# Cross-attention of eight samples to memory: column groups of four samples at a time, key tiles in another order

## The chip, the cores and the metric

The kernel runs on one core of a Trainium2 chip. Its TensorE (PE) multiplies, VectorE (DVE), ScalarE (ACT) and GpSimd (POOL) work on vectors, and DMA queues move data between the chip's main memory and the core's own. The metric is the device time of one execution in microseconds (us).

## What is computed

One inference step of a two-layer decoder, for a prompt of 512 tokens and for eight samples of four tokens each. Both share all weights. Every layer has a token mixer, a cross-attention with four heads into 256 memory rows, and a feed-forward block. The change lies in the cross-attention of the samples. Each sample has its own keys and values, given as inputs (`cache_mem_k`, `cache_mem_v`), and its tokens attend to all 256 of them:

```python
def gqa_attend(q, k, v, mask):
    b, tq, h, dh = q.shape
    g = k.shape[2]
    qg = q.reshape(b, tq, g, h // g, dh)
    s = jnp.einsum('btgod,bsgd->bgots', qg, k).astype(jnp.float32) * (dh ** -0.5)
    s = jnp.where(mask, s, NEG_INF)
    p = jnp.where(mask, jax.nn.softmax(s, axis=-1), 0.0)
    o = jnp.einsum('bgots,bsgd->btgod', p.astype(v.dtype), v)
    return o.reshape(b, tq, h, dh), p

def cross_attend(h, mk, mv, wq, wo):
    b, t, _ = h.shape
    q = (h @ wq).reshape(b, t, XATTN_HEADS, XATTN_HEAD_DIM)
    o, _ = gqa_attend(q, mk, mv, True)
    return o.reshape(b, t, D_MODEL) @ wo
...
        xs = xs + rmsnorm(cross_attend(rmsnorm(xs, gn[2]), cache_mem_k[li], cache_mem_v[li], w_xq[li], w_xo[li]), gn[3])
```

One sample has four heads of four tokens, 16 rows of queries. Its keys of one layer are 8 chunks of 128 by 256, its values 2 chunks of 128 by 1024: 1 MB each.

## The kernel before

The program is written by hand, one list of instructions for each engine, with semaphores between them. Each engine runs its list strictly in the written order.

**PE.** In a layer, `cross(l)` follows the query projection. It works on the prompt (`scores`, `turn`, `values`, in four blocks of 128 queries) and on the samples in turn. For the samples:

- Keys (L1938 to L1944). `xqd[:, b, c, :]` holds the queries of sample b, chunk c, in 32 columns: two samples share one 32-row strip of the result, each filling half of it and leaving zeros in the other. So the result of sample b goes to rows 32*(b//2) of `ps[.., 1, 0:256]`, and the strip sums 16 matmuls: 8 chunks of two samples. A strip of 32 result rows is a column group of PE's array, since the stationary operand has 32 columns. The order is sample by sample: 8 matmuls each, 64 in all, with a rise of `mk_used` after each sample.
- Softmax on DVE and ACT, transposes on PE, and ACT's copy to `xst` (L913).
- Values (`s_values(hb)`, L1915). For the four samples of a half, each in a strip of its own (rows 32*j), two matmuls for each half `f` of the 1024 columns, 512 wide. The order is sample by sample, 4 matmuls each, with a rise of `mv_used` after each. Between the two halves stand blocks 2 and 3 of the prompt's scores and some transposes.

**Tiles.** A key or value tile of a sample is loaded by POOL's DMA queue into one of six places (`NC` = 4 places in the ring `cring` and `XC` = 2 in free space). The list `TILES` (L166 to L173) gives the order of loading, and with it the place: the n-th tile of a layer's keys and values goes to place n mod 6. `tile(n)` waits until the tile before it in the place was used (`tile_used`, L524 to L535), then issues the DMA. POOL does this in the order of the list, between its sums for the norms: the first four tiles of a layer before the norm of the memory, the other twelve after the last projection of the memory's values. PE waits in `tile_in` for the tile's arrival (`cache_full`).

Weights come by another queue (SyncE) into a ring of four blocks. The blocks of the output projection that follows `cross` are requested up to its fourth before `cross` begins.

Of the kernel before, what the change touches and what calls it, by code (L numbers as in the profile page):

```python
# [34 lines left out]
P = 128  # L35
# [3 lines left out]
NB, NT = 8, 4  # L39
# [125 lines left out]
TILES = [("cmp", b, kv, h) for b in range(NB) for kv in "kv" for h in range(2)]  # L165
for _hb in range(2):  # L166
# [2 lines left out]
    TILES += [("win", _hb, "v", 0)]  # L169
    TILES += [("slc", 4 * _hb + j, "k", h) for j in range(2, 4) for h in range(2)]  # L170
    TILES += [("slc", 4 * _hb + j, "v", h) for j in range(4) for h in range(2)]
TILES += [("mem0", b, kv, 0) for kv in "kv" for b in range(NB)]
TILES += [("mem1", b, kv, 0) for kv in "kv" for b in range(NB)]  # L173
TILE = {t: i for i, t in enumerate(TILES)}

XC = 2
# [80 lines left out]
def decoder_step(nc, a, w, o):  # L257

    with ExitStack() as ctx:
# [13 lines left out]
        def S(name):  # L273

            if name not in sems:
                sems[name] = ctx.enter_context(nc.semaphore(name))
            return sems[name]
# [25 lines left out]
        ps = ctx.enter_context(nc.psum_tensor("ps", [P, 8, 512], F32))  # L303
# [66 lines left out]
        xqd = flatx[:, 1280:3328].rearrange("p (b c n) -> p b c n", b=NB, c=8)  # L370
# [69 lines left out]
        def tile_in(e, *t):  # L440

            n = TILE[t]
            e.wait_ge(cfull[PLACE[n]], 16 * TURN[n])
            return place_of(n)
# [71 lines left out]
        def _(pool):  # L516
# [6 lines left out]
            def tile_used(n):  # L523

                kind, b, kv, hh = TILES[n]
                if kind == "cmp":
                    pool.wait_ge(S("sub_ready"), n + 1)
                elif kind == "win":
                    pool.wait_ge(S("sw_sc" if kv == "k" else "sw_pv"), b + 1)
                elif kind == "slc" and kv == "k":  # L530
                    pool.wait_ge(S("kt_tr"), 4 * (2 * b + hh + 1))
                elif kind == "slc":
                    pool.wait_ge(S("sv_used"), 2 * b + hh + 1)
                else:
                    pool.wait_ge(S("mk_used" if kv == "k" else "mv_used"), 8 * int(kind[3]) + b + 1)  # L535

            def tile(n):
                kind, b, kv, hh = TILES[n]
# [37 lines left out]
            k = 0  # L576
            at = NC
# [994 lines left out]
        def _(pe):  # L1572
            pe.wait_ge(S("const_loaded"), 32)

            def mm(out, lhsT, rhs, start, stop, **kw):
                return pe.matmul(out, lhsT, rhs, start=start, stop=stop, **kw)  # L1576
# [83 lines left out]
            for kind, k in FIRST:  # L1660
# [3 lines left out]
                if kind == "in":  # L1664
                    last = plain(g, WSEG["w_in"][0] + k, h, 8, 0, KC, None if k else "h_ready")
# [212 lines left out]
            def cross(l):  # L1878
# [35 lines left out]

                def s_values(hb):  # L1915

                    for j in range(4):
                        b = 4 * hb + j
                        mv = tile_in(pe, f"mem{l}", b, "v", 0)
                        for f in range(2):  # L1920
                            for kt in range(2):
                                at = kt * P + 32 * (b // 2)
                                last = mm(ps[32 * j:32 * j + 32, 6 * hb + f, :], xst[:, at:at + 32],
                                          mv[:, kt * 1024 + 512 * f:kt * 1024 + 512 * f + 512], kt == 0, kt == 1)
                        last.then_inc(S("mv_used"), 1)

                def s_turn(hb):
                    pe.wait_ge(S("xv_copied_a"), 2 * l + hb + 1)
# [6 lines left out]
                scores(0)  # L1935

                pe.wait_ge(S("xq_apart"), l + 1)
                for b in range(NB):  # L1938
                    mk = tile_in(pe, f"mem{l}", b, "k", 0)
                    rows = slice(32 * (b // 2), 32 * (b // 2) + 32)  # L1940
                    for c in range(8):
                        last = mm(ps[rows, 1, 0:256], xqd[:, b, c, :], mk[:, c * 256:c * 256 + 256],
                                  b % 2 == 0 and c == 0, b % 2 == 1 and c == 7)
                    last.then_inc(S("mk_used"), 1)  # L1944
                scores(1)
                turn(0)
                pe.wait_ge(S("xs_norm"), l + 1)
# [195 lines left out]
```

## Time and profile before

| | |
|---|---|
| median of 3 runs | 2154.64 us (2154.55 to 2156.26) |
| span of the profiled execution | 2150.9 us |
| PE busy (share of the span), instructions | 1977.7 us (92%), 13423 |
| PE weight loads | 1734.4 us (81%) |
| VectorE | 1021.7 us (48%) |
| ScalarE | 710.4 us (33%) |
| GpSimd | 255.9 us (12%) |
| DMA queue of GpSimd (q0) | 109.53 MB, 13.7% of 16 engines |

The span is the time from the first to the last instruction of the one execution that was profiled. Its rows below are read from that execution. In them, a form such as "128*32 128x256" is a stationary operand of 128 rows by 32 columns and a moving operand of 128 by 256. `mc` is the memory that holds the ring and more, and stands for the tiles in both keys and values; `big` holds the queries (`xqd`) and the probabilities (`xst`); `kstore` is the prompt's keys, `vstore` its values, `cst` the identity for transposes, `small` other queries of the samples.

### The profile page before, as it was taken

What the parts mean: (1) busy time and instruction counts of PE and PEld (TensorE: products, weight loads), DVE (VectorE), ACT (ScalarE), POOL (GpSimd) and SP (SyncE); (2) the same over time, 40 slices, a digit from 0 to 9 for tenths busy, and PEclk for the clock granted to TensorE, in tenths of its full rate; (3) what the DMA queues carried; (4) which work ended last, traced back from release to release, by engine and by line L of the source; (5) the groups of instructions that cost most, each with busy time, mean ns of one, the idle gap of its engine ahead of it and who ended that gap; (6) DMA issues with size and microseconds to landing.
All of it is one profiled execution on the core that took longest, in us unless ns stands there. A gap on an engine that the chain in (4) does not pass through costs nothing.

```text
span 2150.9 us, 31915 instructions
## 1 busy us (share of the span) xinstructions
PE 1977.7 (92%) x13423; PEld 1734.4 (81%) x13423; DVE 1021.7 (48%) x1429; ACT 710.4 (33%) x1179; POOL 255.9 (12%) x231
## 2 busy tenths in 40 slices
PE   5997999898989997999999979898999899999995
PEld 4785764647979567999999979887965799999995
DVE  5994774242374225544432176755522364444213
ACT  2113553233452144322222232754313332222221
POOL 2340001110230003000000121021200210000011
PEclk8996999999999998999999989999999999999998
DMA  6893005554254511222222222243551222222221
GB/s 227 335 374 139 1 1 196 192 175 162 79 166 147 196 40 49 89 88 87 86 85 87 87 63 82 89 153 128 181 186 41 77 69 88 88 88 85 87 86 59
DMA packets 59656, 254.75 MB, mean 118 GB/s; under 512 B 10224, under 2 KB 10624, under 8 KB 45904
## 3 DMA queue, kind: packets, MB, share of 16 engines
q1 hardware_dynamic: 40320, 135.39, 19.6%
q0 software_dynamic: 14656, 109.53, 13.7%
q10 hardware_dynamic: 4576, 8.34, 1.1%
q8 instruction: 78, 1.28, 0.2%
q14 instruction: 26, 0.21, 0.0%
HBM read 244.89 MB, written 12.68 MB: 120 GB/s over the span
## 4 chain that ended last, share of the span: by engine, by line
PE 81%; DVE 12%; ACT 4%; DMA 1%; issue 1%; POOL 0%; SPq 0%; ACTq 0%; DVEq 0%; POOLq 0%
PE ps L1576 77%; DVE work L1102 3%; PE ps L1838 2%; DVE big L1163 1%; PE ps L1744 1%; DVE work_r L1124 1%; DVE rinv L1086 1%; DVE wring_r L1116 1%; ACT whi L677 1%; DVE x L1105 1%; ACT work L848 1%; DVE mc L1537 0%; DMA cst<-in_const 0%; DMA mc<-in_cmpv,idx 0%; ACT big L882 0%
## 5 line engine op out<-in xcount | busy, mean ns | idle before, releaser
L1576 PE MATMUL ps<-work_r,whi 128*128 128x272 f32 x4352 | 761.1, 292 | 46.9 <-ACT work_r L689 27.6
L1576 PEld LDWEIGHTS ps<-work_r,whi 128*128 128x128 f32 x4352 | 632.3, 191 | 60.7 <-issue 39.9
L1576 PE MATMUL ps<-work_r,wring_r 128*128 128x272 f32 x2432 | 511.2, 292 | 0.0
L677 ACT ACTIVATE whi<-wring 128x1024 fp32r<-128x1024 f32 (+1 forms) x232 | 242.3, 1045 | 788.4 <-PE ps L1576 786.1
L1116 DVE TENSOR_TENSOR wring_r<-wring,whi 128x1024 fp32r<-128x1024 f32 (+1 forms) x232 | 283.7, 1225 | 432.7 <-ACT whi L677 432.5
L1576 PEld LDWEIGHTS ps<-work_r,wring_r 128*128 128x128 f32 x2432 | 387.7, 193 | 0.0
L1576 PE MATMUL ps<-mc_r,whi 128*128 128x272 f32 x1216 | 241.4, 288 | 0.0
L1576 PE MATMUL ps<-big_r,whi 128*128 128x272 f32 (+1 forms) x960 | 197.5, 293 | 13.0 <-DVE wring_r L1116 13.0
L1576 PEld LDWEIGHTS ps<-mc_r,whi 128*128 128x128 f32 x1216 | 187.4, 188 | 0.0
L1576 PEld LDWEIGHTS ps<-big_r,whi 128*128 128x128 f32 x960 | 154.8, 195 | 14.5 <-DVE wring_r L1116 14.3
L1576 PE MATMUL ps<-mc_r,wring_r 128*128 128x272 f32 x704 | 145.7, 288 | 0.0
L1576 PE MATMUL ps<-work,wring 128*128 128x272 f32 x480 | 115.8, 401 | 6.7 <-DVE work L1093 6.7
L1163 DVE TENSOR_REDUCE big<-mc 128x128 f32<-128x2048 f32 x32 | 115.7, 3674 | 10.7 <-DMA mc<-in_cmpk,idx 7.6
L1576 PEld LDWEIGHTS ps<-work,wring 128*128 128x128 f32 x480 | 93.1, 195 | 26.7 <-issue 7.4
L569 POOL TENSOR_TENSOR ssum<-ssum,sq 128x544 f32<-128x544 f32 (+1 forms) x56 | 79.1, 1413 | 259.7 <-ACT sq L654 257.9
L1576 PEld LDWEIGHTS ps<-mc_r,wring_r 128*128 128x128 f32 x704 | 109.9, 189 | 0.0
L569 POOL TENSOR_TENSOR ssum<-sq 128x544 f32<-128x544 f32 (+1 forms) x13 | 18.2, 1401 | 761.1 <-ACT sq L654 761.1
L1454 DVE TENSOR_TENSOR kstore<-ps,rinv 128x544 f32<-128x544 f32 x44 | 31.9, 724 | 151.0 <-PE ps L1576 151.0
L1576 PE MATMUL ps<-mc,big 128*32 128x256 f32 (+1 forms) x384 | 86.1, 452 | 5.3 <-ACT big L913 5.3
L1449 DVE TENSOR_TENSOR big<-ps,rinv 128x544 f32 (+1 forms) x44 | 31.9, 724 | 112.1 <-PE ps L1576 112.0
L1576 PEld LDWEIGHTS ps<-mc,big 128*32 128x32 f32 x384 | 35.4, 110 | 52.8 <-issue 23.3
L1576 PE MATMUL ps<-big,small 128*32 128x512 f32 (+1 forms) x136 | 68.0, 585 | 5.2 <-DVE big L1309 5.2
(291 smaller groups left out, 2196.1 us busy)
## 6 DMA issues: line engine op xcount, KB each, us to landing
wring<-w_ffn SPq DMA_DIRECT2D x88, 512.0 KB, 3.5
mc<-in_memk POOLq DMA_DIRECT2D x16, 1024.0 KB, 5.4
mc<-in_memv POOLq DMA_DIRECT2D x16, 1024.0 KB, 5.1
wring<-w_down SPq DMA_DIRECT2D x32, 512.0 KB, 3.4
wring<-w_w_out SPq DMA_DIRECT2D x16, 512.0 KB, 3.7
wring<-w_mk SPq DMA_DIRECT2D x16, 512.0 KB, 3.5
wring<-w_mv SPq DMA_DIRECT2D x16, 512.0 KB, 4.1
wring<-w_xq SPq DMA_DIRECT2D x16, 512.0 KB, 3.5
```

What stands on the lines that cost most here:

```text
L569: pool.tensor_tensor(ssum[:, 0:wd], sq[:, 0, 0:wd] if c == 1 else ssum[:, 0:wd], sq[:, c % 2, 0:wd], ALU.add).then_inc(S("sq_summed"), 1)
L677: act.activation(dst, src, ACT.Copy).then_inc(S("w_hi"), 1)
L848: act.activation(piece, piece, ACT.Exp, bias=sst[:, 3 * hb + 2, 1:2], scale=SC, accum_out=sxs[:, k:k + 1]).then_inc(S("sx_exp"), 1)
L1086: dve.reciprocal(rinv[:, 0:wd], rms[:, 0:wd]).then_inc(S("rinv_ready"), 1)
L1102: dve.tensor_tensor(y[:, c, :], y[:, c, :], rinv[:, :], ALU.mult).then_inc(S("y_scaled"), 1)
L1105: dve.tensor_tensor(x[:, c - 1, :], x[:, c - 1, :], y[:, c - 1, :], ALU.add).then_inc(S("x_ready1"), 1)
L1116: dve.tensor_tensor(lo, src, F(hi), ALU.subtract).then_inc(S("w_lo"), 1)
L1163: dve.tensor_reduce(subs[:, n % 8, :], src.rearrange("p (r c) -> p c r", r=SUB), AXX, ALU.add).then_inc(S("sub_ready"), 1)
L1449: dve.tensor_tensor(halves(hid[j]), accp[g % 4], halves(rinv[:, :]), ALU.mult).then_inc(drained[g % 4], 1)
L1454: dve.tensor_tensor(halves(uprow[:, j, :]), accp[g % 4], halves(rinv[:, :]), ALU.mult).then_inc(drained[g % 4], 1)
L1576: return pe.matmul(out, lhsT, rhs, start=start, stop=stop, **kw)
L1838: last = pe.transpose(ps[:, n % 2, r * P:r * P + P], kt_[:, at:at + P], ident)
```

## The change

The tile list loads a layer's keys in the order of samples 0, 2, 4, 6, then 1, 3, 5, 7 (`MEMK`), and `tile_used` counts a key tile by its place in that order. Values are loaded in the order 0 to 7, as before. PE takes the keys in two batches of four samples, one in each strip; within a batch it goes chunk by chunk, and for each chunk through the four strips. It waits for the batch's four tiles ahead of its first matmul, and raises `mk_used` in the batch's last round, once for each sample. `s_values` takes its four samples in the same way: for each `f` and `kt`, through the four strips.

```diff
--- before.py
+++ after.py
@@ -169,8 +169,11 @@
     TILES += [("win", _hb, "v", 0)]
     TILES += [("slc", 4 * _hb + j, "k", h) for j in range(2, 4) for h in range(2)]
     TILES += [("slc", 4 * _hb + j, "v", h) for j in range(4) for h in range(2)]
-TILES += [("mem0", b, kv, 0) for kv in "kv" for b in range(NB)]
-TILES += [("mem1", b, kv, 0) for kv in "kv" for b in range(NB)]
+
+MEMK = [2 * q + e for e in range(2) for q in range(4)]
+for _l in range(2):
+    TILES += [(f"mem{_l}", b, "k", 0) for b in MEMK]
+    TILES += [(f"mem{_l}", b, "v", 0) for b in range(NB)]
 TILE = {t: i for i, t in enumerate(TILES)}
 
 XC = 2
@@ -532,7 +535,8 @@
                 elif kind == "slc":
                     pool.wait_ge(S("sv_used"), 2 * b + hh + 1)
                 else:
-                    pool.wait_ge(S("mk_used" if kv == "k" else "mv_used"), 8 * int(kind[3]) + b + 1)
+                    at_ = MEMK.index(b) if kv == "k" else b
+                    pool.wait_ge(S("mk_used" if kv == "k" else "mv_used"), 8 * int(kind[3]) + at_ + 1)
 
             def tile(n):
                 kind, b, kv, hh = TILES[n]
@@ -1914,15 +1918,15 @@
 
                 def s_values(hb):
 
-                    for j in range(4):
-                        b = 4 * hb + j
-                        mv = tile_in(pe, f"mem{l}", b, "v", 0)
-                        for f in range(2):
-                            for kt in range(2):
-                                at = kt * P + 32 * (b // 2)
+                    mvs = [tile_in(pe, f"mem{l}", 4 * hb + j, "v", 0) for j in range(4)]
+                    for f in range(2):
+                        for kt in range(2):
+                            for j in range(4):
+                                at = kt * P + 32 * ((4 * hb + j) // 2)
                                 last = mm(ps[32 * j:32 * j + 32, 6 * hb + f, :], xst[:, at:at + 32],
-                                          mv[:, kt * 1024 + 512 * f:kt * 1024 + 512 * f + 512], kt == 0, kt == 1)
-                        last.then_inc(S("mv_used"), 1)
+                                          mvs[j][:, kt * 1024 + 512 * f:kt * 1024 + 512 * f + 512], kt == 0, kt == 1)
+                                if f and kt:
+                                    last.then_inc(S("mv_used"), 1)
 
                 def s_turn(hb):
                     pe.wait_ge(S("xv_copied_a"), 2 * l + hb + 1)
@@ -1935,13 +1939,14 @@
                 scores(0)
 
                 pe.wait_ge(S("xq_apart"), l + 1)
-                for b in range(NB):
-                    mk = tile_in(pe, f"mem{l}", b, "k", 0)
-                    rows = slice(32 * (b // 2), 32 * (b // 2) + 32)
+                for e in range(2):
+                    mks = [tile_in(pe, f"mem{l}", 2 * q + e, "k", 0) for q in range(4)]
                     for c in range(8):
-                        last = mm(ps[rows, 1, 0:256], xqd[:, b, c, :], mk[:, c * 256:c * 256 + 256],
-                                  b % 2 == 0 and c == 0, b % 2 == 1 and c == 7)
-                    last.then_inc(S("mk_used"), 1)
+                        for q in range(4):
+                            last = mm(ps[32 * q:32 * q + 32, 1, 0:256], xqd[:, 2 * q + e, c, :],
+                                      mks[q][:, c * 256:c * 256 + 256], e == 0 and c == 0, e == 1 and c == 7)
+                            if c == 7:
+                                last.then_inc(S("mk_used"), 1)
                 scores(1)
                 turn(0)
                 pe.wait_ge(S("xs_norm"), l + 1)
```

How this moves PE's instructions shows in two places. The first is PE's list at the keys of layer 0, before, from the third sample's tile in place 3 to the prompt's second block of scores; `cache_full0` to `cache_full5` are the arrivals in the six places:

```order
L1576 MATMUL ps<-mc,big 32x256 [waits cache_full3]
L1576 MATMUL ps<-mc,big 32x256 x7
L1576 MATMUL ps<-mc,big 32x256 [waits cache_full4]
L1576 MATMUL ps<-mc,big 32x256 x7
L1576 MATMUL ps<-mc,big 32x256 [waits cache_full5]
L1576 MATMUL ps<-mc,big 32x256 x7
L1576 MATMUL ps<-mc,big 32x256 [waits cache_full0]
L1576 MATMUL ps<-mc,big 32x256 x7
L1576 MATMUL ps<-mc,big 32x256 [waits cache_full1]
L1576 MATMUL ps<-mc,big 32x256 x7
L1576 MATMUL ps<-kstore,big 128x256 [waits xp_exp]
L1576 MATMUL ps<-kstore,big 128x256 x7
```

The same stretch now, from the prompt's first block of scores on:

```order
L1580 MATMUL ps<-kstore,big 128x256 x7
L1580 MATMUL ps<-mc,big 32x256 [waits cache_full2,cache_full1,cache_full3,cache_full0,xq_apart]
L1580 MATMUL ps<-mc,big 32x256 x31
L1580 MATMUL ps<-mc,big 32x256 [waits cache_full0,cache_full1,cache_full5,cache_full4]
L1580 MATMUL ps<-mc,big 32x256 x31
L1580 MATMUL ps<-kstore,big 128x256 [waits xp_exp]
L1580 MATMUL ps<-kstore,big 128x256 x7
```

The eight waits for one tile each have become two waits for four tiles, with 32 matmuls behind each; places 0 and 1 are waited for a second time ahead of the second batch, together with places 4 and 5.

The second place is the first half of the values, before, from the transposes of the samples' probabilities (`rms`) to the prompt's next scores:

```order
L1949 MATMUL ps<-cst,rms 128x128 [waits xs_norm]
L1949 MATMUL ps<-cst,rms 128x128
L1576 MATMUL ps<-mc,big 32x512 [waits cache_full2,xs_trc]
L1576 MATMUL ps<-mc,big 32x512 x3
L1576 MATMUL ps<-mc,big 32x512 [waits cache_full3]
L1576 MATMUL ps<-mc,big 32x512 x3
L1576 MATMUL ps<-mc,big 32x512 [waits cache_full4]
L1576 MATMUL ps<-mc,big 32x512 x3
L1576 MATMUL ps<-mc,big 32x512 [waits cache_full5]
L1576 MATMUL ps<-mc,big 32x512 x3
L1576 MATMUL ps<-kstore,big 128x256 [waits xp_exp]
L1576 MATMUL ps<-kstore,big 128x256 x7
```

And now:

```order
L1954 MATMUL ps<-cst,rms 128x128 [waits xs_norm]
L1954 MATMUL ps<-cst,rms 128x128
L1580 MATMUL ps<-mc,big 32x512 [waits cache_full4,cache_full3,cache_full5,cache_full2,xs_trc]
L1580 MATMUL ps<-mc,big 32x512 x15
L1580 MATMUL ps<-kstore,big 128x256 [waits xp_exp]
L1580 MATMUL ps<-kstore,big 128x256 x7
L1903 MATMUL ps<-cst,big 128x128 [waits xp_trc,xp_norm]
L1903 MATMUL ps<-cst,big 128x128 x7
```

Here four waits with four matmuls behind each have become one wait for four tiles with 16 matmuls behind it. POOL's list is the same in both kernels, with other samples' keys in it.

## Rows read from the trace of the kernel before

**Rows 1.** The page: the chain that ended last, shares of the span by engine

```profile
PE 81%; DVE 12%; ACT 4%; DMA 1%; issue 1%; POOL 0%; SPq 0%; ACTq 0%; DVEq 0%; POOLq 0%
```

**Rows 2.** Groups by form, PE: line, engine, form, count | busy us, mean ns | idle

```profile
L1576 PE MATMUL ps<-mc,big 128*32 128x256 f32 x256 | 50.6, 380 | 0.0
...
L1576 PE MATMUL ps<-mc,big 128*32 128x512 f32 x128 | 35.4, 595 | 5.3 <-ACT big L913 5.3
...
L1576 PE MATMUL ps<-mc,work 128*32 128x128 f32 x256 | 27.9, 273 | 0.0
...
L1576 PE MATMUL ps<-mc,small 128*32 128x512 f32 x16 | 2.1, 592 | 0.0
```

**Rows 3.** Timeline of PE, layer 0: start us, length us, merged group [idle before <-releaser]

```profile
699.87 25.31 PE L1576 MATMUL ps<-mc,big 128*32 128x256 f32 x128
725.12 3.72 PE L1576 MATMUL ps<-kstore,big 128*128 128x256 f32 x16
...
732.60 8.86 PE L1576 MATMUL ps<-mc,big 128*32 128x512 f32 x32 [2.67 <-ACT big L913]
741.39 3.72 PE L1576 MATMUL ps<-kstore,big 128*128 128x256 f32 x16
...
753.12 8.86 PE L1576 MATMUL ps<-mc,big 128*32 128x512 f32 x32
761.91 1.09 PE L1899 MATMUL ps<-cst,big 128*128 128x128 f32 x8
```

**Rows 4.** Timeline of PE, layer 1

```profile
1576.64 25.31 PE L1576 MATMUL ps<-mc,big 128*32 128x256 f32 x128
...
1609.36 8.86 PE L1576 MATMUL ps<-mc,big 128*32 128x512 f32 x32 [2.67 <-ACT big L913]
```

**Rows 5.** Timeline of PE: window scores of the samples, two rounds of four groups

```profile
325.15 1.04 PE L1576 MATMUL ps<-mc,small 128*32 128x512 f32 x8
```

**Rows 6.** Timeline of weight loads: window scores, then first half of the values

```profile
324.94 0.35 PEld L1576 LDWEIGHTS ps<-mc,small 128*32 128x32 f32 x8
...
733.91 0.11 PEld L1576 LDWEIGHTS ps<-mc,big 128*32 128x32 f32 x1 [0.32 <-issue]
734.34 0.14 PEld L1576 LDWEIGHTS ps<-mc,big 128*32 128x32 f32 x3 [0.32 <-issue]
734.77 0.14 PEld L1576 LDWEIGHTS ps<-mc,big 128*32 128x32 f32 x2 [0.29 <-issue]
```

**Rows 7.** Timeline of POOL's queue, layer 0

```profile
703.81 0.53 POOL L551 DMA_DIRECT2D mc<-in_memk  x1 [54.75 <-PE ps L1576]
707.27 0.53 POOL L551 DMA_DIRECT2D mc<-in_memk  x1 [2.93 <-PE ps L1576]
...
725.49 0.53 POOL L551 DMA_DIRECT2D mc<-in_memv  x1 [2.93 <-PE ps L1576]
```

**Rows 8.** Tile loads by POOL: of 700 to 730; 1413 to 1415, first two, last two

```profile
DMA to landing us min/median/max: 5.0/5.0/5.1
...
L551 POOL DMA_DIRECT2D mc<-in_memk x4: 535/548/593, 1413.4 to 1415.0; - x4
...
DMA to landing us min/median/max: 5.4/6.3/7.2
...
DMA to landing us min/median/max: 9.2/10.7/12.1
```

**Rows 9.** Windows around a stop of PE in layer 1: busy us, granted clock PEclk

```profile
core 0: us, PE busy (x) PEld busy (x) DVE busy (x) ACT busy (x) POOL busy (x), PEclk, DMA share, GB/s
1371.30:1376.50 5.20, 0.04 (x2) 0.05 (x1) 4.93 (x15) 5.05 (x8) 0.00 (x0) 0.93 0.33 101
1376.50:1380.00 3.50, 3.50 (x15) 3.50 (x16) 3.45 (x6) 3.47 (x6) 0.00 (x0) 0.50 0.00 0
1380.00:1383.00 3.00, 3.00 (x16) 3.00 (x16) 2.83 (x5) 2.51 (x4) 0.00 (x0) 0.56 0.00 0
```

**Rows 10.** Timeline of VectorE (DVE), layer 0: last step on the softmax's fourth block

```profile
756.00 1.23 DVE L1403 TENSOR_TENSOR big<-big,small 128x1024 f32<-128x1024 f32 x1
```


## The prediction

> **What bounds the kernel now.** I read the chain of work that ended last first: 81% of it is TensorE (PE) [rows 1], so whatever shortens PE's own sequence comes off the end, as long as PE has nothing else to wait for. Next the groups of PE by form, for what the change touches: the matmuls of the samples' keys, 128x32 weights by 256 columns, 256 records, 50.6 us in all, and those of the values, 128x32 by 512, 128 records, 35.4 us [rows 2]. The program has half as many matmuls: each f32 matmul is two records, a weight load and a pass each time ("a pair" below). Then PE's timeline of layer 0. It shows keys 699.87 to 725.12 (25.25 us), 7.48 us up to the values of the first four samples, these 8.79 us, 11.73 us to the second half, 8.79 us again [rows 3]. Layer 1 has the same lengths, 25.31 and 8.86 us busy [rows 4]. No wait for a tile stands in either stretch. So 42.8 us per layer are at stake.
>
> **What one group of columns costs.** In the values, weight loads follow each other every 0.43 us, which is the pace of one 512-wide pair in one column group; two or three loads together at 734.34 and 734.77 show the next sample, in another column group, starting while the first one's last pairs still wait their turn [rows 6]. That is why 32 pairs take 8.79 and not 13.8 us: the old order already overlaps at the three changes of group. A 256-wide pair then has a pace of 0.215 us (half).
>
> **What four groups at a time cost.** The kernel has this form in two other places, the scores of compressed and window keys, where four samples follow each other in four groups. There eight 512-wide records (two rounds of four) take 1.04 us from first start to last end, and one record alone is 0.59 [rows 2, 5]: all eight start within 0.45 us. One after the other they would take 8 x 0.43 = 3.4 us. So four groups run at once, at one round in 0.43 us (512) or 0.215 us (256). What these rows don't show is that pace kept up for long: they are 8 pairs.
>
> **Keys.** A batch is now four samples x 8 chunks = 32 matmuls, 64 pairs, 16 rounds: 16 x 0.215 = 3.44 us, as long as one sample took before. The first batch reads the four places that were filled long ago. The reloads go by GpSimd's (POOL's) queue, in a row of waits on mk_used. Before, the first place came free after one sample: the DMA was issued at 703.81, 3.94 us after the keys began, the next at 707.27 [rows 7]. Now all four places come free at that same 703.8, and four tiles of 1 MB are issued 0.53 us apart: two keys, then two values. PE's second batch needs four tiles at once, two of which are these two keys. That wait is new; before, the seventh key tile was wanted some 19 us after the start. Queued behind it on PE is the rest of the kernel.
>
> The price of the wait: four tiles issued together stand in the trace before layer 1's keys, at 1413.4 to 1415.0. The first two landed 5.4 and 7.2 us after their own issue, the last two 9.2 and 12.1 us [rows 8]; from the first issue that is 5.4, 7.8, 10.3 and 13.7 us. A tile alone takes 5.0 to 5.1 us [rows 8]. The second key tile so lands at 703.8 + 7.8 = 711.6, and PE stands for 8 us from 703.6.
>
> The price of the clock: after a stop of 5.2 us the granted clock was 0.50 for the next 3.5 us and 0.56 over the 3 us behind that, with PE busy all the time [rows 9]: some 6.1 us at 1.2 instead of 2.4 GHz. In 6.1 us the batch does 3.05 of its 3.44 us of work, so it takes 6.5 us (bounds: 3.44 with no fall, 6.9 with the low level throughout). Keys end at 711.6 + 6.5 = 718.1 instead of 725.1. **Gain 7.0 us.** Had only the matmuls mattered it would be 18.4.
>
> **Values, first half.** The next four value tiles go out when the second batch is done, 0.4 us later as now (725.12 to 725.49 [rows 3, 7]): 718.5. The two value tiles issued earlier landed by 703.8 + 13.7 = 717.5, so the queue is empty. The first half wants the second of the four: 718.5 + 7.8 = 726.3. PE's own work between keys and values (scores, two sets of transposes, 2.67 us of waiting for ScalarE's copy [rows 3]) is untouched, 7.48 us, and ends at 725.6. Wait 0.7 us. Work 8 rounds x 0.43 = 3.44 instead of 8.79. **Gain 5.35 - 0.7 = 4.65 us.**
>
> **Values, second half.** Its last two tiles go into places that the first half frees at 729.8; the queue is busy until 718.5 + 13.7 = 732.2, two more at the 2.4 to 3.4 us steps of [rows 8] land by 739. PE comes at 729.8 + 11.73 = 741.5: no wait, 2.5 us to spare. Behind it stand transposes that want the fourth block of the prompt's softmax: VectorE's last step on it ends at 757.23, 4.1 us after the second half began [rows 10]. The 8.79 us hid it; 3.44 do not. Wait 0.7 us. **Gain 4.65 us.** From there on all is as before, earlier.
>
> **Sum.** 7.0 + 4.65 + 4.65 = 16.3 us per layer, 32.6 us for two. The profiled execution's span is 2150.9 us, the median of the runs 2154.64, so 3.7 us lie around the span and stay. 2150.9 - 32.6 = 2118.3 in the span, 2122.0 for the run. The other edits have one answer: the number of instructions is the same, the key tiles are the same bytes in another order, and the semaphores rise as often.
>
> **A rule against it.** In the window scores the eight weight loads fill 0.35 us in all, from 324.94 on [rows 6], where one load alone takes 0.11; they don't follow one another. The Trainium skill, "TensorE: Matmul & The Clock Gate", Part 3 on packing small matmuls, says that a weight load overlaps running matmuls only where its row group differs; here all four use all 128 rows. By that rule the 0.11 us loads would follow one another, which is rival B's result; this trace disagrees with it for 8 pairs and is silent beyond.
>
> **Rivals.**
> A, the sum above, own range 2117 to 2127 (clock and landing a little either way).
> B, a pair can't start more often than every 0.11 us, by its loads or by PE's supply of instructions. For: the fastest long stream with 32-column weights is 27.9 us for 256 pairs, 0.109 each [rows 2], and the 8 pairs of [rows 5] may have stood ready in a queue. Against: [rows 5, 6]. A batch then takes 64 x 0.109 = 7.0 us: 3.6 us more for the first, 0.5 for the second (it ran slow anyway), nothing for values, whose pace is 0.107. 4.1 per layer: 2130.
> C, tiles issued together land together, at 13.7 us. For: the four share 16 DMA engines. Against: the steps in [rows 8]. Keys would end at 717.5 + 6.5 = 724.0 (gain 1.1), values wait 6.6 us (loss 1.2), the second half 2.5 us (gain 2.1): 2.0 per layer, 2151.
> D, the clock doesn't fall, or only at the end of the batch: 3.0 more gained per layer, 2116. Against: it fell after shorter stops [rows 9].
> E, **slower**: the groups don't run at once in this form, since four tiles' data stream into one array from one memory. Then a batch is 64 x 0.215 = 13.8 us. The reloads are issued at 714.1, the second lands at 721.9, the second batch ends at 738.7 with 3 us of low clock: 13.6 lost. Each half of values costs 13.8 instead of 8.8, 5 more. 23.6 per layer: 2202. It decides from fewer than 1.8 matmuls at a time: with n at once the two batches and two halves cost 4 x 13.8/n, and 12.7 come on top (8.3 stop, 3.0 clock, 1.4 waits), against 42.8 now. [rows 5] show four.
>
> **How the numbers follow.** A 0.62, B 0.14, D 0.10, C 0.05, E 0.03, and 0.06 for a gain that something later takes back in part (2133 to 2150). Likeliest: 2122.0. The range must hold A, B and D, and B with a tile that lands 1 us late: 2114 to 2133; outside are C, E and the last case, 0.14. A measurement of this kernel tells 0.2% (4.3 us) from no change. Faster by that: all but E and most of C, 0.94; within: 0.03; slower: 0.03.
>
> **What would show it.** Keys: two blocks of 64 records on PE, the first 3.4 to 3.8 us, a stop near 8 us ended by a DMA, the second over 5 us at clock 0.5. A first block of 7 us is B, of 14 E. A stop over 12 us is C; a clock near 1.0 behind the stop is D. On POOL four issues in 1.6 us where 3 us lay between. Values: 32 records in 3.5 to 3.7 us, each half; a short stop ended by a DMA before the first, and by VectorE behind the second. I am wrong if the stop of PE between the batches is far from 8 us, or if PE waits for a tile before the second half.

## The result and the profile after

The changed kernel takes 2122.34 us (median of 4 runs, 2115.77 to 2126.86) against 2155.18 us (4 runs, 2154.55 to 2156.26) of the kernel before. The ratio is 0.9841, with a 95% interval from 0.9818 to 0.9865. Forecast were 2122.0 us. The profiled execution has a span of 2113.8 us, 37.1 us less than before; it is the quickest of the four.

PE's groups by form show what the matmuls themselves lost, against the first two lines of [rows 2]:

```profile
L1580 PE MATMUL ps<-mc,big 128*32 128x256 f32 x256 | 19.9, 481 | 16.4 <-DMA mc<-in_memk 16.4
...
L1580 PE MATMUL ps<-mc,big 128*32 128x512 f32 x128 | 14.6, 595 | 6.3 <-DMA mc<-in_memv 6.3
```

The same 256 and 128 records now fill 19.9 and 14.6 us instead of 50.6 and 35.4. That would be 51.5 us. But both groups now have idle time before them, 16.4 us until a key tile and 6.3 us until a value tile has landed, where [rows 2] have 0.0 and 5.3.

The page's chain names the same two, 1% each, with PE's share at 80 instead of 81 [rows 1]:

```profile
PE 80%; DVE 11%; ACT 4%; DMA 3%; issue 1%; POOL 0%; SPq 0%; ACTq 0%; DVEq 0%; POOLq 0%
...
PE ps L1580 76%; DVE work L1106 3%; PE ps L1842 2%; DVE big L1167 1%; PE ps L1748 1%; DVE rinv L1090 1%; DVE wring_r L1120 1%; ACT whi L681 1%; DMA mc<-in_memk 1%; DVE x L1109 1%; DMA mc<-in_memv 1%; ACT work L852 1%; DVE mc L1541 0%; DMA cst<-in_const 0%; DMA mc<-in_cmpv,idx 0%
```

PE's timeline of layer 0 after the change answers to [rows 3]. Columns as there: start, length, group, idle time before it:

```profile
696.25 3.66 PE L1580 MATMUL ps<-mc,big 128*32 128x256 f32 x64
708.06 6.22 PE L1580 MATMUL ps<-mc,big 128*32 128x256 f32 x64 [8.15 <-DMA mc<-in_memk]
714.21 3.72 PE L1580 MATMUL ps<-kstore,big 128*128 128x256 f32 x16
...
722.20 3.64 PE L1580 MATMUL ps<-mc,big 128*32 128x512 f32 x32 [3.17 <-DMA mc<-in_memv]
725.77 3.72 PE L1580 MATMUL ps<-kstore,big 128*128 128x256 f32 x16
...
737.50 3.64 PE L1580 MATMUL ps<-mc,big 128*32 128x512 f32 x32
741.65 1.09 PE L1903 MATMUL ps<-cst,big 128*128 128x128 f32 x8 [0.51 <-DVE big L1407]
```

The keys go from 696.25 to 714.21, 17.96 us instead of 25.25: a batch of 3.66 us, a stop of 8.15 us that a key tile's DMA ends, and a batch of 6.22 us, the same 64 records again. The first half of the values takes 3.57 us (to 725.77) instead of 8.79, behind a stop of 3.17 instead of 2.67 us. The second takes 3.64, and behind it stands the new wait for VectorE, 0.51 us. In layer 1 ([rows 4] before):

```profile
1555.97 3.66 PE L1580 MATMUL ps<-mc,big 128*32 128x256 f32 x64
1567.84 6.41 PE L1580 MATMUL ps<-mc,big 128*32 128x256 f32 x64 [8.20 <-DMA mc<-in_memk]
...
1582.17 3.64 PE L1580 MATMUL ps<-mc,big 128*32 128x512 f32 x32 [3.18 <-DMA mc<-in_memv]
...
1597.47 3.64 PE L1580 MATMUL ps<-mc,big 128*32 128x512 f32 x32
```

POOL's queue shows the four issues in a row that [rows 7] had 3 us apart, and how long the first two, then all four, took to land:

```profile
700.19 1.05 POOL L555 DMA_DIRECT2D mc<-in_memk  x2 [54.76 <-PE ps L1580]
701.23 1.04 POOL L555 DMA_DIRECT2D mc<-in_memv  x2
...
DMA to landing us min/median/max: 5.1/6.1/7.2
...
DMA to landing us min/median/max: 5.1/8.2/11.1
```

The second, issued at 700.7, took 7.2 us and landed at 707.9; PE went on at 708.06. Windows over the stop, the second batch, and the first half of the values give the granted clock (third from the end):

```profile
core 0: us, PE busy (x) PEld busy (x) DVE busy (x) ACT busy (x) POOL busy (x), PEclk, DMA share, GB/s
699.90:708.06 8.16, 0.01 (x2) 0.03 (x1) 1.28 (x2) 0.00 (x0) 2.08 (x4) 0.69 0.80 309
708.06:714.20 6.14, 6.14 (x64) 3.14 (x64) 0.00 (x0) 0.00 (x0) 0.00 (x0) 0.57 0.64 272
722.20:725.77 3.57, 3.57 (x33) 1.10 (x33) 0.63 (x1) 0.00 (x0) 0.00 (x0) 1.00 1.03 431
```

0.57 over the second batch, 1.00 over the values.

### The profile page after: what moved, and what is told of

The parts are those of the page before. It is cut to its first block, busy times and chain, and to the rows that moved or that the text cites. A ratio compares the mean times of both kernels' runs of the same rounds, so it can differ in the third digit from the quotient of the medians.

```text
span 2113.8 us, 31927 instructions
## 1 busy us (share of the span) xinstructions
PE 1920.9 (91%) x13423; PEld 1710.1 (81%) x13423; DVE 1021.1 (48%) x1429; ACT 709.9 (34%) x1179; POOL 256.3 (12%) x231
## 3 DMA queue, kind: packets, MB, share of 16 engines
q1 hardware_dynamic: 40320, 135.39, 19.9%
q0 software_dynamic: 14656, 109.53, 13.8%
## 4 chain that ended last, share of the span: by engine, by line
PE 80%; DVE 11%; ACT 4%; DMA 3%; issue 1%; POOL 0%; SPq 0%; ACTq 0%; DVEq 0%; POOLq 0%
PE ps L1580 76%; DVE work L1106 3%; PE ps L1842 2%; DVE big L1167 1%; PE ps L1748 1%; DVE rinv L1090 1%; DVE wring_r L1120 1%; ACT whi L681 1%; DMA mc<-in_memk 1%; DVE x L1109 1%; DMA mc<-in_memv 1%; ACT work L852 1%; DVE mc L1541 0%; DMA cst<-in_const 0%; DMA mc<-in_cmpv,idx 0%
## 5 line engine op out<-in xcount | busy, mean ns | idle before, releaser
L573 POOL TENSOR_TENSOR ssum<-sq 128x544 f32<-128x544 f32 (+1 forms) x13 | 18.2, 1399 | 743.5 <-ACT sq L658 743.5
L1327 DVE TENSOR_TENSOR work<-ps,big 32x512 f32<-32x512 f32 x64 | 44.0, 687 | 52.6 <-PE ps L1580 51.1
L839 ACT ACTIVATE big<-ps 128x512 f32<-128x512 f32 x64 | 37.9, 596 | 68.7 <-PE ps L1842 68.7
```

Of the source, the lines that this page charges most:

```text
L573: pool.tensor_tensor(ssum[:, 0:wd], sq[:, 0, 0:wd] if c == 1 else ssum[:, 0:wd], sq[:, c % 2, 0:wd], ALU.add).then_inc(S("sq_summed"), 1)
L839: act.activation(ktb[:, n % 2, :], ps[:, n % 2, :], ACT.Copy).then_inc(S("kt_trc"), 1)
L1327: dve.tensor_tensor(sslc[rows, at:at + 512].rearrange("p (r b s) -> p r b s", r=4, s=4), ps[rows, 2 + n % 2, :].rearrange("p (r b s) -> p ...
```

## Where the time between two profiles lies

The time from the first key matmul to the prompt's own values (`ps<-big,vstore`) is the stretch that holds all that the change touches. It is read from PE's timeline; before it was 63.96 and 63.91 us in the two layers. In the profile after it is 47.32 and 47.53. That is 33.0 of the 37.1 us. The other 4.1 lie in code that both kernels share: ahead of the first keys (the head below), 699.87 before and 696.25 after, 3.62 less, and between the layers, 812.80 and 812.40. The first and second windows of before, then of after, show the same instructions and the clock:

```profile
0.00:699.87 699.87, 619.10 (x3631) 474.44 (x3631) 401.58 (x694) 238.73 (x504) 122.03 (x123) 0.94 0.47 169
763.84:1576.64 812.80, 767.17 (x5606) 736.12 (x5605) 391.50 (x471) 294.21 (x385) 88.38 (x65) 0.97 0.29 94
```

```profile
0.00:696.25 696.25, 614.29 (x3632) 470.23 (x3632) 401.30 (x694) 238.28 (x504) 122.71 (x123) 0.95 0.47 170
743.57:1555.97 812.40, 766.99 (x5605) 736.72 (x5604) 391.32 (x471) 294.22 (x385) 88.20 (x65) 0.97 0.29 94
```

Over all profiles of this study the head lasts 693.4 to 701.8 us, at a mean clock of 0.96 in the shortest and 0.94 in the longest. So up to 8 us of difference between two spans can come from the head, which the change doesn't touch. The single runs of one kernel lie 2 to 15 us apart, those of before too (2148.1 to 2161.8 beside e_order); only the profiled one of each can be taken apart, so where the spread of the others lies is not shown. The stretch from the keys to the prompt's values is the sharper measure, and the experiments are read by it (where an expectation counts to the transposes behind the second half of the values, that end lies 1.9 us earlier, two sets of transposes):

| kernel | layer 0 | layer 1 | median us | ratio to before |
|---|---|---|---|---|
| before | 63.96 | 63.91 | | |
| e_order | 60.62 | 60.58 | 2147.54 | 0.9968 [0.9951, 0.9985] |
| e_keys | 56.54 | 56.30 | 2136.41 | 0.9923 [0.9901, 0.9946] |
| e_values | 55.81 | 55.76 | 2134.73 | 0.9920 [0.9894, 0.9945] |
| after | 47.32 | 47.53 | 2122.34 | 0.9841 [0.9818, 0.9865] |
| after, again (r_after) | 47.16 | 47.40 | 2122.25 | 0.9857 [0.9833, 0.9881] |
| e_warm | 46.21 | 46.36 | 2118.09 | 0.9831 [0.9805, 0.9857] |
| e_two | 46.01 | 45.99 | 2113.99 | 0.9814 [0.9791, 0.9838] |
| e_warm2 | 44.76 | 44.59 | 2107.6 (1 run) | |
| e_eight | 41.96 | 41.89 | 2107.58 | 0.9803 [0.9767, 0.9840] |
| e_eight_swap | 39.03 | 41.50 | 2102.70 | 0.9784 [0.9744, 0.9824] |

Each ratio is to the kernel before, run again beside the experiment: 2152.45 us (8 runs) beside e_keys, e_values, e_two and e_warm, 2154.67 us (7 runs) beside r_after, e_warm2, e_eight and e_eight_swap, 2153.68 us (9 runs) beside e_order. The three groups ran on three chips, so medians compare best within a group.

## The experiments

**One part alone: e_keys and e_values.** In e_keys the values keep their old loop, in e_values the keys and the load order keep theirs.

> The keys in two batches of four groups and their load order, as in the changed kernel; the values sample by sample, as before. Theory (stop for two key tiles): the key stretch lasts 18.0 us instead of 25.25 us per layer, of which about 8.2 us are the stop and 6.2 us a second batch at the low clock; 0.5 us of that goes to the tile wait ahead of the values. 6.8 us per layer, 13.6 us in all: 2141.6 us. Rival (the pace of four groups is all that counts, the stop is an accident of one profile): 18.4 us per layer, 2118 us.

Measured: keys from 696.60 to 714.42, 17.8 us, with a stop of 7.86 and a second batch of 6.30 us.

```profile
696.60 3.66 PE L1580 MATMUL ps<-mc,big 128*32 128x256 f32 x64
708.12 6.37 PE L1580 MATMUL ps<-mc,big 128*32 128x256 f32 x64 [7.86 <-DMA mc<-in_memk]
714.42 3.72 PE L1580 MATMUL ps<-kstore,big 128*128 128x256 f32 x16
...
721.90 8.86 PE L1580 MATMUL ps<-mc,big 128*32 128x512 f32 x32 [2.67 <-ACT big L917]
```

The median is 2136.41 us (expected 2141.6; the kernel before beside it was 2.7 us under the 2155.18 of the result). 7.4 and 7.6 us per layer are gained in the stretch, a little more than the 6.8 expected, because no tile wait shows ahead of the values (2.67 us, ScalarE's, as before). 18.4 us per layer, the rival's figure, is out. The stop is there in both layers (7.91 us in layer 1), so it is no accident of one profile.

> The values by four groups at a time; the keys and the load order as before. Theory: 5.2 us gained in the first half and 4.6 us in the second (0.5 us wait for VectorE's last step of the fourth block), no wait for a tile in either: 9.9 us per layer, 19.7 us in all, 2135.5 us. Rival (value tiles come too late as soon as the first half is shorter): a stop ended by a DMA before the second half, less than 5 us per layer, over 2145 us.

Measured: 8.15 us per layer instead of 9.9, and no stop by a DMA ahead of the second half. The second half took 3.64 us as expected. The first took 5.34:

```profile
731.19 5.34 PE L1576 MATMUL ps<-mc,big 128*32 128x512 f32 x32 [2.67 <-ACT big L913]
736.46 3.72 PE L1576 MATMUL ps<-kstore,big 128*128 128x256 f32 x16
...
748.19 3.64 PE L1576 MATMUL ps<-mc,big 128*32 128x512 f32 x32
```

In layer 1 it took 5.27 us again. The windows over the stop and the half show why: 0.68 of the clock. In e_keys the same stop of 2.67 us left the clock at 1.00.

```profile
728.50:731.19 2.69, 0.02 (x1) 0.00 (x0) 0.62 (x4) 2.64 (x11) 0.00 (x0) 1.00 0.03 9
731.19:736.46 5.27, 5.27 (x33) 1.29 (x33) 1.14 (x1) 0.00 (x0) 0.00 (x0) 0.68 0.00 0
```

```profile
719.20:721.90 2.70, 0.03 (x2) 0.00 (x1) 0.63 (x4) 2.65 (x11) 0.00 (x0) 1.00 1.04 431
721.90:730.69 8.79, 8.79 (x32) 2.39 (x33) 1.14 (x1) 0.00 (x0) 1.05 (x2) 1.00 0.95 354
```

The median of e_values, 2134.73 us, meets the 2135.5 expected by luck: the stretches gave 16.3 us of the 19.7 expected, and the kernel before beside it was 2.7 us quicker.

So the two parts give 7.5 + 8.2 = 15.7 us per layer, and both together 16.5. Three differences make this up: the low clock cost e_values 1.7 us in this half, which the profile after did not pay; the changed kernel pays a tile wait of 0.5 us ahead of it and 0.3 us more in its keys, which the parts alone don't.

**The load order alone: e_order.** Keys sample by sample in the new order, values as before. The tile list and `tile_used` are those of the changed kernel; PE's loop is, in part:

```diff
-                for b in range(NB):
-                    mk = tile_in(pe, f"mem{l}", b, "k", 0)
...
+                for e in range(2):
+                    for q in range(4):
+                        mk = tile_in(pe, f"mem{l}", 2 * q + e, "k", 0)
```

> The new load order alone: keys sample by sample in the order 0, 2, 4, 6, 1, 3, 5, 7, values sample by sample. Theory: the order costs nothing and brings nothing, 63.9 us in each layer from the start of the keys to the prompt's values, as before, less what more frequent changes of the column group let overlap: seven changes instead of three, 0.4 to 0.7 us at each, 2 to 3 us per layer; no stop between the samples. 2150 us. Rival (the order itself is what gives part of the changed kernel's gain, apart from four groups at a time): over 5 us per layer.

Measured: 3.3 us per layer, a little over the 2 to 3 expected and under the rival's 5, and 0.9968 of the time before. The keys take 21.91 us instead of 25.25, with nothing idle:

```profile
700.86 21.98 PE L1580 MATMUL ps<-mc,big 128*32 128x256 f32 x128
722.77 3.72 PE L1580 MATMUL ps<-kstore,big 128*128 128x256 f32 x16
```

Seven changes of column group instead of three save 3.34 us, 0.84 for each further change: the time of four 256-wide pairs. The weight loads of before agree. In the values one load comes every 0.43 us within a sample; at the first change there are three, two and two, the first two of which [rows 6] show and the third of which is

```profile
735.20 0.14 PEld L1576 LDWEIGHTS ps<-mc,big 128*32 128x32 f32 x2 [0.29 <-issue]
```

That makes four loads more than one at a time. My estimate had been 0.4 to 0.7. So a fifth of the gain in the changed kernel was to be had by the order alone.

**Two groups at a time: e_two.**

```diff
-                    mks = [tile_in(pe, f"mem{l}", 2 * q + e, "k", 0) for q in range(4)]
-                    for c in range(8):
-                        for q in range(4):
-                            last = mm(ps[32 * q:32 * q + 32, 1, 0:256], xqd[:, 2 * q + e, c, :],
-                                      mks[q][:, c * 256:c * 256 + 256], e == 0 and c == 0, e == 1 and c == 7)
-                            if c == 7:
-                                last.then_inc(S("mk_used"), 1)
+                    for q0 in range(0, 4, 2):
+                        mks = [tile_in(pe, f"mem{l}", 2 * q + e, "k", 0) for q in range(q0, q0 + 2)]
+                        for c in range(8):
+                            for q in range(q0, q0 + 2):
+                                last = mm(ps[32 * q:32 * q + 32, 1, 0:256], xqd[:, 2 * q + e, c, :],
+                                          mks[q - q0][:, c * 256:c * 256 + 256], e == 0 and c == 0, e == 1 and c == 7)
+                                if c == 7:
+                                    last.then_inc(S("mk_used"), 1)
```

> The changed kernel, but the keys go through two column groups at a time: samples 0 and 2, then 4 and 6, then 1 and 3, then 5 and 7, 3.4 us each. The matmuls of the keys then take 13.8 us per layer instead of 6.9. Theory (the reload of two tiles sets the end of the keys, and the clock falls in the long stop): the first places come free as early as now, three pairs of samples fill the 7.8 us until the second tile lands but for 1.4 us, the clock stays at the high level, and the last pair takes 3.4 us: keys in 15.2 us instead of 18.0, no tile wait ahead of the values. 3.3 us per layer gained on the changed kernel: 2115.7 us. Rival (the number of groups at a time sets the time): 6.9 us per layer lost on the changed kernel, 2136 us.

Measured: 2113.99 us (expected 2115.7), and 46.0 us in both layers, less than the 47.3 of four groups at a time, though the keys' matmuls take longer.

```profile
697.26 8.90 PE L1580 MATMUL ps<-mc,big 128*32 128x256 f32 x96
708.81 3.65 PE L1580 MATMUL ps<-mc,big 128*32 128x256 f32 x32 [2.65 <-DMA mc<-in_memk]
712.39 3.72 PE L1580 MATMUL ps<-kstore,big 128*128 128x256 f32 x16
...
720.19 5.34 PE L1580 MATMUL ps<-mc,big 128*32 128x512 f32 x32 [2.99 <-DMA mc<-in_memv]
```

Three pairs of samples take 8.90 us (less than 3 x 3.44; e_order's overlap at a change of groups would explain it, but this was not looked at by itself), a stop of 2.65 us follows, ended by the DMA of a key tile again, and the last pair takes 3.58 us at the full clock: 15.13 us, expected 15.2. The rival wanted 6.9 us more per layer than the changed kernel; it falls. The end of the keys is set by the reload, and what the stop does to the clock comes on top. Here too the first half of the values took 5.3 us at clock 0.68; without that the gain on the changed kernel would be about the 3 us per layer of the forecast. With it the stretch shows 1.3 and 1.5 us, 2.9 in all. The median lies 8 us under the changed kernel's, more than the stretch accounts for, and the two intervals of the ratio overlap: that two groups are quicker than four rests on the stretch.

**Work inside the stop: e_warm and e_warm2.** Both compute the same as the changed kernel. The added matmuls write to a part of PSUM (the memory that takes PE's results) that nobody reads.

```diff
+                    if e:
+                        for _ in range(16):
+                            mm(ps[:, 0, 0:256], C("ident"), kstore[:, 0, :], True, True)
```

> The changed kernel, with 16 matmuls whose result nobody reads (128 rows, 128x128 by 256, into a free part of PSUM) between the two key batches: 7.1 us of work inside the stop of 8.2 us. Theory (part of the price is TensorE's clock after the stop): the second batch takes 3.7 us instead of 6.2 to 6.4 at a granted clock near 1.0; 2.6 us per layer, 5.2 us in all: 2117.1 us. Rival (the second batch is slow because its tiles still arrive or the groups share a limit): nothing gained, 2122 us. If the runs of the changed kernel spread over 11 us because of the clock behind the stops, the runs of this one lie closer together, within some 3 us as those of the kernel before; if not, as wide as before.

```profile
core 0: us, PE busy (x) PEld busy (x) DVE busy (x) ACT busy (x) POOL busy (x), PEclk, DMA share, GB/s
705.36:713.37 8.01, 7.18 (x36) 6.03 (x33) 1.35 (x2) 0.00 (x0) 2.08 (x4) 1.00 0.77 312
713.37:716.96 3.59, 3.59 (x64) 2.36 (x64) 0.00 (x0) 0.00 (x0) 0.00 (x0) 1.00 1.00 424
724.91:730.18 5.27, 5.27 (x33) 1.56 (x33) 0.67 (x1) 0.00 (x0) 0.00 (x0) 0.68 0.78 330
```

The second batch takes 3.59 us at clock 1.00 instead of 6.15 at 0.57: 2.56 us, expected 2.6. Its four tiles are the same, and they landed just as late (PE waits 0.83 us more behind the filling). In layer 1 it is 3.59 us at 1.00 too. So the long second batch is the clock behind the stop and nothing else. But the stretch is only 1.1 to 1.2 us shorter, since the first half of the values now fell into the low clock (0.68) in both layers, which it had not in the profile after. So the two layers give 2.3 us of the 5.2 expected, and the median of 2118.09 us meets the expected 2117.1 by luck; by their ratios the two kernels can't be told apart. The runs did not come closer together (2113.4 to 2123.3): the clock behind this stop does not account for the spread. That part of the expectation was wrong.

e_warm2 adds six such matmuls in the 3 us ahead of the values:

```diff
+                for _ in range(6):
+                    mm(ps[:, 6, 0:256], C("ident"), kstore[:, 0, :], True, True)
```

> The changed kernel with idle matmuls in both stops: 16 between the key batches, and 6 (2.7 us) ahead of the first half of the values, where the kernel with the first filling alone took 5.3 us for that half instead of 3.6. Theory (a stop of 3 us ahead of it lets the clock fall or not, by chance): the first half takes 3.6 us in both layers at clock 1.0; 42.7 us from the start of the keys to the transposes. Rival (the first half is slow because its tiles still arrive): 5.3 us again.

```profile
705.00:708.59 3.59, 3.59 (x65) 2.36 (x65) 0.00 (x0) 0.00 (x0) 0.00 (x0) 1.00 1.00 422
716.79:720.36 3.57, 3.57 (x32) 1.10 (x32) 0.42 (x1) 0.00 (x0) 0.00 (x0) 1.00 1.02 429
```

Both at 1.00, 3.59 and 3.57 us; to the transposes 42.8 and 42.7 us, as expected. The rival (5.3 us again) falls. About 2.7 us per layer of the changed kernel's time, then, are the price of a slow clock behind its stops; the stops themselves are the price of the tiles. (The 2107.6 us of this single run flatter it: its head is the shortest of all, 693.4 us.)

**Without the reload: e_eight.** Two more places, in the half of `work` that is free from the end of the query projection on. Their arrivals are counted on two semaphores that the program uses once at its start, `pages_loaded` and `pool_past`.

```diff
+                m = n - TILE[kind, 0, "k", 0]
+                s = m if m < 8 else (0, 1, 4, 5, 2, 3, 6, 7)[m - 8]
...
+        yflat = y.rearrange("p c t -> p (c t)")
...
+        cfull = [S(f"cache_full{s}") for s in range(NC + XC)] + [S("pages_loaded"), S("pool_past")]
...
+            if s >= NC + XC:
+                return yflat[:, (s - NC - XC) * 2048:(s - NC - XC) * 2048 + 2048]
...
+                    if n == n0 + NC + XC:
+                        acc_done(pool, acc_of(f"xq{l}", 7))
```

> The changed kernel with eight places for tiles instead of six: the last two keys of a layer go into the free upper half of `work` as soon as the query projection has read it, so no key tile is loaded behind a used one. The values take places 0, 1, 4, 5, 2, 3, 6, 7. Theory (the whole rest of the price is the stop and the clock behind it): no stop between the batches, keys in 7.2 us per layer instead of 18.0; the wait for the fourth value tile ahead of the first half then grows to about 4.6 us in all (2.67 of it for ScalarE's copy, as ever), and the first half may take 5.3 us at the low clock. From start of keys to the transposes 37.8 us instead of 45.4: 15 us in all, 2107 us. Rival (the tiles' bandwidth sets the time, the stop only moves behind the keys): a wait of over 10 us ahead of the values, 2120 us or more.

Measured: 41.96 and 41.89 us, 2107.58 us. The keys take 7.76 us in layer 0, from 696.23 to 703.99, with 0.51 us idle between the batches; PE then stops ahead of the values for 5.86 us, ended by a value tile, and the first half takes 5.72 us at a clock of 0.62. In layer 1 the keys take 8.94 us, with 1.69 us idle until a key tile has landed, the stop is 4.23 us and the first half takes 6.13 us at 0.58.

```profile
696.23 3.66 PE L1592 MATMUL ps<-mc,big 128*32 128x256 f32 x64
...
703.99 3.72 PE L1592 MATMUL ps<-kstore,big 128*128 128x256 f32 x16
...
714.66 5.79 PE L1592 MATMUL ps<-mc,big 128*32 128x512 f32 x32 [5.86 <-DMA mc<-in_memv]
720.38 3.72 PE L1592 MATMUL ps<-kstore,big 128*128 128x256 f32 x16
...
1570.58 6.20 PE L1592 MATMUL ps<-mc,big 128*32 128x512 f32 x32 [4.23 <-DMA mc<-in_memv]
```

In layer 0 that is 10.2 us fewer for the keys and 4.8 us more ahead of and in the first half: 5.4 us net, where 7.6 were expected (to the transposes 40.0 us, not 37.8). The missing 2.2 us are 1.3 in the stop (5.86, not 4.6), 0.6 in the keys (7.76, not 7.2) and 0.4 in the first half (5.72, not 5.3). The median met the expected 2107 us all the same, by luck: it lies 14.7 us under r_after's, the stretches 10.7. The rival (over 10 us ahead of the values) falls, but half of it is true: once the keys don't wait, PE waits for the value tiles.

**And the wait for the values covered: e_eight_swap.**

```diff
+                scores(2)
                 pe.wait_ge(S("xs_trc"), l + 1)
                 s_values(0)
-                scores(2)
```

> The kernel with eight places, and on TensorE the prompt's third block of scores ahead of the first half of the values instead of behind it. Theory: the scores start when the second block's exponentials are done, 14.2 us after the keys began, and fill the wait for ScalarE's copy and for the fourth value tile; the rest follows 4.0 us behind the first half instead of 7.2 behind it. 34.1 us instead of 37.8 per layer, 7 us in all: 2100 us. Rival (the softmax of the third block becomes the bound, since VectorE's list has the copy of the first half ahead of it): the stop only moves to the fourth block's scores, 2107 us.

```profile
710.28 3.72 PE L1592 MATMUL ps<-kstore,big 128*128 128x256 f32 x16 [2.40 <-ACT big L898]
713.94 3.64 PE L1592 MATMUL ps<-mc,big 128*32 128x512 f32 x32
...
721.77 5.41 PE L1592 MATMUL ps<-kstore,big 128*128 128x256 f32 x16 [2.15 <-ACT big L898]
727.01 1.04 PE L1915 MATMUL ps<-cst,big 128*128 128x128 f32 x8
```

The third block's scores now stand where PE waited, and the first half of the values follows them at once, at 3.57 us. To the transposes it is 37.1 us in layer 0 and 39.6 in layer 1, against 34.1 expected. The fourth block's scores start 4.3 us behind the first half (4.0 expected), but took 5.24 us instead of 3.56 here, again behind a stop (2.15 us), and the keys had lost 0.9 us to a stop of 0.80 us between the batches. Layer 1 lost 2.5 us more ahead of the first half: 1.63 us idle between the batches instead of 0.80, and the third block's scores took 5.34 us at a clock of 0.68 behind the same stop of 2.40 us that left them at 3.66 in layer 0. So of the 7 us expected the stretches show 2.9 and 0.4. Neither side held: the scores cover the wait for the value tiles, but most of the gain was lost again, in good part to the low clock behind the stops of 2.15 and 2.40 us that are left. At 2102.70 us this is the quickest version that was run, 0.9784 [0.9744, 0.9824] of the time before and 20 us under the changed kernel run beside it (r_after), 14 of them in the stretches.

**The changed kernel again: r_after.**

> The changed kernel once more, beside the next three. Theory: from the start of the keys to the transposes behind the second half of the values 45.4 us in each layer (62.0 before), give or take 2 us where the stop of about 3 us ahead of the values is followed by a low clock or not; 2122 us, with the runs some 8 us apart, since other stretches of the program differ from run to run by the same cause.

It came back at 2122.25 us, to the transposes 45.2 and 45.5 us. In layer 1 its second batch took 4.8 us and the first half 5.3 us, in layer 0 6.3 and 3.6: the low clock falls on one or the other, and the sum hardly moves.

## Why the prediction was right

**The bound.** PE's list set the time, and what it lost came off the end. From the start of layer 1's own values of the prompt to the end the span has 510.35 us before and 510.30 after.

**Four groups at a time.** The first batch is busy for 3.66 us, the last matmul's 0.4 us to its end included; 3.44 were forecast to the start of what follows, and at full clock that took 3.59 us (e_warm). The pace that [rows 5] showed for 8 pairs holds for 64. Rival B (a pair every 0.11 us, 7.0 us for a batch, which is also what "A rule against it" came to) and rival E (no overlap, 13.8 us) fall by that line alone.

**The stop.** The second key tile was forecast 7.8 us behind the first issue, by [rows 8], and landed 7.7 us behind it; the stop was 8.15 us, forecast 8. Rival C (all land together) falls by the two keys' landings, 5.1 and 7.2 us behind their own issues. One reading of [rows 8] was loose: the 5.0 to 5.1 us of "a tile alone" are those of loads issued about 3.5 us apart, each of which still ran beside the next. No term hangs on it.

**The clock.** Second batch: 6.5 us forecast, 6.15 and 6.34 measured in the two layers, at 0.57 and 0.56. e_warm shows that it is the clock. Rival D falls.

**Keys in all**: 18.2 us forecast (699.87 to 718.1), 17.96 and 18.21 measured. **First half**: a wait of 0.7 us for the tile forecast, 0.5 measured (PE went on 7.6 us behind the first of POOL's four issues, forecast 7.8); 3.44 forecast for the work, 3.57 measured. **Second half**: no tile wait, as forecast (in layer 0 the last tile landed at 733.8, PE came for it at 737.5), and 0.7 forecast against 0.51 measured for VectorE. Per layer a gain of 16.3 us was forecast, 16.6 and 16.4 were measured.

**What the sum did not hold** is that executions differ by more than its terms are off. The median met the forecast within 0.4 us, which is luck: the single runs lie between 2115.8 and 2126.9, and the profiled one was 4 us quicker outside the changed stretch than the profile before. What is not luck is that each term was met within 0.4 us in the stretch. The range of 2114 to 2133 had been made of the rivals' prices, and happened to hold this too. Nor did it hold the first half of the values at a low clock, which costs 1.7 us per layer in e_values, e_two, e_warm and r_after's layer 1; in the last a shorter second batch paid for it.

**What the sum implied and I had not drawn out**: the matmuls of the keys fell by 18 us per layer and the time by 7; 11 us went into the stop and the clock behind it. Half the overlap was enough: e_two, which has it, is 1.3 to 1.5 us per layer quicker in the stretch.

## What to carry to other kernels

Taking several inputs at once shortens the matmuls, but it also gives all their buffers back at once, at the end: count how many tiles the next batch still lacks, and when the first of its places comes free. If the reload takes longer than the batch, two groups at a time can beat four (e_two, by a little over 1 us per layer here): they free the first places just as early, 3.9 us after the start of the keys in both, and keep PE at work while these are filled, and two more places beat both (e_eight). A stop can cost more than its length: add a low clock behind it to its price, and check by harmless work in the gap whether it is the clock or the data that makes the next stretch slow.

## What the runs showed of the hardware that I had not expected

Stops of PE of 2.1 to 3.2 us were followed by the low clock in some places and not in others, and their length does not tell which. Behind 2.15 us the prompt's scores ran at 0.67 (e_eight_swap, both layers), behind 2.65 us e_two's last keys ran at 1.00. After 2.67 us, ended by the same ScalarE copy, the clock was 0.68 over the next 5.3 us in e_values, and 1.00 in before, e_order and e_keys. The same half of the values takes 3.6 us or 5.3 us by that.

It is not mere chance from one execution to the next either, as I had expected it to be. Ahead of the first half of the values, the two layers of a profile agree in every kernel but r_after. With the values sample by sample, the clock stayed at 1.00 in 6 of 6 cases. With four groups at a time, and stops of 2.7 to 3.1 us, it was 0.68 in all 6 where the keys ahead had run at full clock (e_values, e_warm, e_two). It stayed at 1.00 in the 3 where the second batch had just run at 0.56 to 0.57 (after, and r_after's layer 0). In r_after's layer 1 the second batch ran at 0.74 and the half at 0.67. So e_warm's work in the first stop moved the low clock behind the second, in both layers, and e_warm2 had to fill both. Why it goes this way, these runs don't show.

Column groups overlap even when the program goes through them one after the other: each further change of group saved 0.84 us with 256 columns, the time of four pairs (e_order).
